# Layer 3's modulation rows: from TensorE fillers in layer 1's attention to GpSimd sums in layer 2's attention

## The reference, cut to what matters

```
shift, scale, gate = jnp.split(jax.nn.silu(c) @ ada_w + ada_b, 3, axis=-1)   # layers 1 and 2; again with c_ctx
h = rmsnorm(x, g_norm) * (1 + scale) + shift
x = x + gate * mixer(h)
...
mod = jax.nn.silu(c_2) @ w_ada[l] + b_ada[l]                                 # layer 3
```

## Time and profile before

| | |
|---|---|
| median of 3 runs (lowest, highest) | 1166.13 us (1163.79, 1166.4) |
| span of the profiled execution, first to last instruction | 1164.7 us |
| busy TensorE / VectorE / ScalarE / GpSimd | 95% / 62% / 56% / 36% |
| chain that ended last | TensorE 77%, VectorE 10%, ScalarE 5%, issue 3%, GpSimd 3%, DMA 2% |
| DMA | 109.33 MB, mean 94 GB/s |
| layer 1's attention | about 103 to 404 us |
| layer 2's attention | about 571 to 753 us |

### The profile page before, as it was taken

One profiled execution on the slowest core, in us unless ns is written; L12 is line 12 of the kernel. 1 busy time (PEld: TensorE's weight loads), 2 busy tenths in 40 slices (PEclk: granted clock), 3 DMA queues, 4 the chain that ended last, 5 costly groups with the idle time before them and its releaser, 6 DMA issues.

```text
span 1164.7 us, 20187 instructions
## 1 busy us (share of the span) xinstructions
PE 1102.9 (95%) x7408; PEld 899.2 (77%) x7408; DVE 726.2 (62%) x1584; ACT 652.1 (56%) x1363; POOL 416.5 (36%) x513
## 2 busy tenths in 40 slices
PE   4899999999998899999999999999999999999996
PEld 0587787878886589888688887798878777888785
DVE  5475665766668725463688788745766775427745
ACT  4614455545556525653577777846567753457733
POOL 1643112111220243676400001416653335456781
PEclk9899999999999999999999999999999999999999
DMA  8732343513113631131201101052312404213112
GB/s 353 270 144 64 111 171 104 187 64 145 46 28 122 228 105 37 37 108 38 57 10 37 64 10 36 13 164 72 87 37 87 150 19 127 91 55 117 47 37 73
DMA packets 34253, 109.33 MB, mean 94 GB/s; under 512 B 4516, under 2 KB 7076, under 8 KB 33772
## 3 DMA queue, kind: packets, MB, share of 16 engines
q1 hardware_dynamic: 34156, 108.05, 27.6%
HBM read 101.39 MB, written 2.11 MB: 89 GB/s over the span
## 4 chain that ended last, share of the span: by engine, by line
PE 77%; DVE 10%; ACT 5%; issue 3%; POOL 3%; DMA 2%; SPq 0%; POOLq 0%; DVEq 0%; ACTq 0%
PE PS L675 31%; PE PS L658 15%; PE PS L791 8%; PE PS L779 7%; PE PS L975 6%; PE PS L1043 3%; PE PS L710 2%; DMA AF<-wstream 2%; PE PS L876 1%; PE PS L691 1%; DVE AD L2364 1%; ACT AF L1267 1%; POOL AR L2545 1%; DVE AF L1982 1%; POOL AR L2561 1%
## 5 line engine op out<-in xcount | busy, mean ns | idle before, releaser
L2545 POOL TENSOR_TENSOR AR<-AF,AR 128x256 fp32r<-128x256 f32 x396 | 301.7, 797 | 596.3 <-ACT AR L1144 596.3
L675 PE MATMUL PS<-AR 128*128 128x512 f32 (+1 forms) x2208 | 450.4, 360 | 4.7 <-POOL AR L2545 1.4
L675 PEld LDWEIGHTS PS<-AR 128*128 128x128 f32 x2208 | 364.0, 189 | 71.8 <-issue 9.7
L658 PE MATMUL PS<-AR 128*128 128x256 f32 (+4 forms) x1284 | 245.5, 327 | 6.7 <-ACT AF L1267 1.7
L658 PEld LDWEIGHTS PS<-AR 128*128 128x128 f32 (+1 forms) x1284 | 180.3, 190 | 42.1 <-issue 21.7
L1276 ACT ACTIVATE AF<-PS 128x512 f32<-128x512 f32 (+3 forms) x192 | 124.6, 649 | 101.1 <-PE PS L779 97.0
L1267 ACT ACTIVATE AF<-PS,AF 128x512 f32<-128x512 f32 (+3 forms) x192 | 140.8, 734 | 27.1 <-DVE AF L2341 18.3
L779 PE MATMUL PS<-AF 128*128 128x128 f32 x864 | 127.7, 275 | 8.3 <-DVE AF L1982 5.7
L1144 ACT ACTIVATE AR<-AF 128x1024 fp32r<-128x1024 f32 x99 | 103.4, 1052 | 41.4 <-PE PS L975 27.9
L779 PEld LDWEIGHTS PS<-AF 128*128 128x128 f32 x864 | 100.2, 140 | 32.6 <-issue 15.5
L791 PE MATMUL PS<-AF 128*64 128x128 f32 x1728 | 115.8, 279 | 3.1 <-DVE AF L1989 2.2
(11 more groups left out here) (213 smaller groups left out, 1136.4 us busy)
## 6 DMA issues: line engine op xcount, KB each, us to landing
AF<-wstream SPq DMA_DIRECT2D x171, 512.0 KB, 5.1
AF<-x_in SPq DMA_DIRECT2D x2, 1024.0 KB, 8.9
AD<-rows SPq DMA_DIRECT2D x4, 512.0 KB, 5.8
out<-AF SPq DMA_DIRECT2D x16, 128.0 KB, 1.9
AF<-AF SPq DMA_DIRECT2D x28, 64.0 KB, 2.0
AF<-rpb_band SPq DMA_DIRECT2D x8, 224.0 KB, 4.9
BIAS<-rpb_band SPq DMA_DIRECT2D x8, 224.0 KB, 4.7
AF<-ctx_in SPq DMA_DIRECT2D x1, 1024.0 KB, 5.8
```

The costliest lines, as they stand in the source:

```text
L658: mm = pe.matmul(out, stationary, moving, start=i == 0, stop=i == len(products) - 1)
L675: mm = pe.matmul(out[:, 0:t1 - t0], a, b, start=k == 0 and i == 0, stop=k == nk - 1 and i == 2)
L2545: ins = pool.tensor_tensor(w[:, 1, at:at + 256], raw(c)[:, at:at + 256], w[:, 0, at:at + 256].bitcast(F32), ALU.subtract)
```

## The change

Layer 3's six blocks leave layer 1's attention. Their chunks stand in the stream behind layer 2's projections, ahead of B.o0. GpSimd takes them one by one: it multiplies each half chunk (128x512) by silu(c_2) of its 128 inputs (one number a partition), adds the two halves, and adds the sum to the block's total (`MIXED`), so that what is left is a sum over the 128 partitions. In step 19 of layer 2's attention TensorE makes that sum for all six blocks (`mixed_rows`, six matmuls with a stationary tile of ones in two columns), VectorE copies it, and the turning `ada2.5.t` follows in step 23. The totals lie where the weight ring for B.o0 to B.o2 is, so ScalarE waits for the turning before it writes these. Layer 2's six blocks are spread anew: one in each of pairs 1, 2, 3 and 5, two in the tail in halves. The roped queries of pairs 2 to 7 move to other places in SyncE's list. Cut:

```diff
 N_CONST = 2
-ADA_GROUPS = {0: ((0, 2), (1, 3), (4, 5)), 1: (tuple(range(6)),), 2: ((0, 1, 2), (3, 4, 5))}
+ADA_GROUPS = {0: ((0, 2), (1, 3), (4, 5)), 1: (tuple(range(6)),), 2: (tuple(range(6)),)}
...
         split(f"A.q{p}", f"A.g{p}")
-        for name in (late_a(p - 1), between_a(p)):
-            if name and not name.endswith(".t"):
-                ada(int(name[3]), int(name[5]))
-    ada(2, 2)
+        name = between_a(p)
+        if name:
+            ada(int(name[3]), int(name[5]))
     split("A.o0")
-    for late in (3, 4, 5):
-        ada(2, late)
+    for late in (4, 5):
+        ada(1, late)
...
           "B.uv", "B.g6", "B.g7", "B.uq1")
+    for b in range(6):
+        ada(2, b)
...
-    return (None, "ada1.0", "ada1.2", "ada1.4", "ada1.5.t", "ada2.1", None, None)[p]
...
-def late_a(p):
-    return (None, "ada1.1", "ada1.3", "ada1.5", "ada2.0", None, None, "ada2.2")[p]
+    return (None, "ada1.0", "ada1.1", "ada1.2", None, "ada1.3", None, None)[p]
...
         late = [f"A.o0.1:{k}" for k in ("02", "24", "45", "56", "67")]
-        return [["ada2.2.t"], ["ada2.3"], ["ada2.4"], ["ada2.5"], ["ada2.5.t"], late[0:1], late[1:3],
+        return [["ada1.4:0"], ["ada1.4:1"], ["ada1.5:0"], ["ada1.5:1"], ["ada1.5.t"], late[0:1], late[1:3],
                 late[3:5]][6 * (p - N_PAIR) + step]
-    gate, between, late = f"A.g{p}.x", between_a(p), late_a(p)
+    gate, between = f"A.g{p}.x", between_a(p)
     out += [[between], [gate]] if between else [[gate + ":0"], [gate + ":1"]]
-    return (out + [[late] if late else []])[step]
+    return (out + [[]])[step]
...
     if step == 3:
-        return []
+        return {5: ["mix2.sum"], 6: ["ada2.5.t"]}.get(p, [])
...
         OB = [tiles(R1, KD, S), tiles(R1[:, KD * S:], KD, S)]
+        MIX = nc.alloc_sbuf_tensor_at("MIX", [P, 7 * S], F32, offset=AR_BASE + 4 * (12288 + 3840 + 6144))
+        MIXED = tiles(MIX, 6, S)
+        ONE_ROW = SILW[:, 0, 0]
...
-            return LOC_[:, 5376:5888]
+            return MIX[:, 6 * S:7 * S] if layer == 2 else LOC_[:, 5376:5888]
...
         sp_x2, ada_used = sem("x_in2"), sem("modulation_chunk_used")
+        mix_step = sem("weighted_rows_step")
...
-        ada_order = [name[:-2] for name, _ in chunks if name.startswith("ada") and name.endswith(".0") and name.count(".") == 2]
+        ada_order = [name[:-2] for name, _ in chunks if name.startswith(("ada0", "ada1")) and name.endswith(".0") and name.count(".") == 2]
+        MIX_STEPS = 6 * 15 + 1
+        def mix_freed(n):
+            halves_added = 1 + 3 * (n + 1) + n - (n + 3) // 4
+            return halves_added + (0 if n % 4 == 0 else 3 if n < 23 else 1)
...
-            def ada_rows(layer, b):
+            def ada_rows(layer, b, k0=0, k1=KD):
                 name = f"ada{layer}.{b}"
-                out = acc_open(name)
+                out = acc_open(name) if k0 == 0 else bank[tasks[name][0]]
                 pe.wait_ge(silc_done, 1)
-                for k in range(KD):
+                for k in range(k0, k1):
...
                         mm.then_inc(ada_used, 1)
-                acc_close(mm, name)
+                if k1 == KD:
+                    acc_close(mm, name)
+            def mixed_rows():
+                out = acc_open("mix2.sum")
+                pe.wait_ge(mix_step, MIX_STEPS)
+                for b in range(6):
+                    g = b % 4
+                    mm = pe.matmul(out[32 * g:32 * g + 12, :], ONE_ROW[:, 10 - 2 * b:22 - 2 * b], MIXED[:, b],
+                                   start=b < 4, stop=b >= 2)
+                acc_close(mm, "mix2.sum")
...
                 out = acc_open(name)
-                rows, i = tasks[f"ada{layer}.{b}"]
+                rows, i = tasks["mix2.sum" if layer == 2 else f"ada{layer}.{b}"]
...
                     project(name, "A.o0", OA, H, T, ready=out_ready(0), k0=int(k[0]), k1=int(k[1]))
+                elif name.startswith("ada") and ":" in name:
+                    piece = int(name[-1])
+                    ada_rows(int(name[3]), int(name[5]), 4 * piece, 4 * piece + 4)
+                elif name == "mix2.sum":
+                    mixed_rows()
...
                             old = in_ring[r - N_SPLIT]
+                            if name in ("B.o0", "B.o1", "B.o2"):
+                                b, i = tasks["ada2.5.t"]
+                                act.wait_ge(acc_ready[b], i)
...
             def ada_part(name):
+                if name == "mix2.sum":
+                    read(dve.tensor_copy(ada_buffer(2, 5), wait_acc(name)), name)
+                    return
...
                 pool.tensor_tensor(QRL[:, i, :], QR[:, i, :], QRH[:, i, :].bitcast(F32), ALU.subtract).then_inc(qr_lo, 1)
+            def mix_rows():
+                b, i = tasks["B.v.5.1"]
+                pool.wait_ge(acc_ready[b], i)
+                done = 1
+                pool.memset(ONE_ROW[:, 10:12], 1.0).then_inc(mix_step, 1)
+                summed = None
+                for b in range(6):
+                    for q in range(4):
+                        c = chunk_at[f"ada2.{b}.{q}"]
+                        w = tiles(raw(c), 2, S)
+                        pool.wait_ge(*raw_loaded(c))
+                        for r in range(2):
+                            pool.tensor_scalar(w[:, r], w[:, r], SILW[:, 1, 2 * q + r, 10:11], None,
+                                               ALU.mult).then_inc(mix_step, 1)
+                        scaled = done + 2
+                        done = scaled
+                        if summed:
+                            add_to(*summed)
+                            done += 1
+                        pool.wait_ge(mix_step, scaled)
+                        total = MIXED[:, b] if q == 0 else w[:, 0]
+                        ins = pool.tensor_tensor(total, w[:, 0], w[:, 1], ALU.add)
+                        ins.then_inc(mix_step, 1)
+                        done += 1
+                        assert q or done == mix_freed(4 * b)
+                        summed = (b, w[:, 0], done) if q else None
+                add_to(*summed)
+                assert done + 1 == MIX_STEPS == mix_freed(23)
+            def add_to(b, part, done):
+                pool.wait_ge(mix_step, done)
+                pool.tensor_tensor(MIXED[:, b], MIXED[:, b], part, ALU.add).then_inc(mix_step, 1)
+            need("B.uq1", 1)
+            mix_rows()
...
                     rows, q = name[:name.rindex(".")], int(name[-1])
-                    if q < 3:
+                    if name.startswith("ada2"):
+                        sp.wait_ge(mix_step, mix_freed(4 * int(name[5]) + q))
+                    elif q < 3:
...
                         sp.wait_ge(acc_ready[b], i)
+            TURN_BEFORE = ("A.g2", "A.g3", "A.g4", "ada1.3.3", "A.g6", "ada1.4.2", "ada1.5.0")
...
                     sp.dma_start(MASK, cst[:, 704:1600]).then_inc(mask_in, 16)
-                for p, before in enumerate(("A.g2", "A.g3", "A.g4", "ada2.0.3", "A.g6", "ada2.2.3", "ada2.3.0"), 1):
+                for p, before in enumerate(TURN_BEFORE, 1):
...
-                if name == "B.o0":
+                if name == "ada2.1.0":
...
                     load_roped_queries(1)
-                for first, after in ((2, "B.o1"), (4, "B.o2"), (6, "B.o5")):
+                for pairs, after in (((2,), "ada2.2.2"), ((3,), "ada2.4.0"), ((4,), "ada2.5.3"), ((5,), "B.o3"), ((6, 7), "B.o5")):
                     if name == after:
-                        load_roped_queries(first)
-                        load_roped_queries(first + 1)
+                        for p in pairs:
+                            load_roped_queries(p)
```

More of the change, by code:

```diff
@@ L247, in filler_chunks @@
         return [f"{name}.{q}" for q in range(4)] if name.count(".") == 1 else []
-    if name.endswith(".rot"):
+    if name.endswith(".rot") or name == "mix2.sum":
         return []
@@ L1447, in evacs_b @@
                     for name in fillers_b(p, s):
-                        if not name.startswith("ada"):
+                        if name[0] == "B":
                             evac_b(name)
@@ L2172, in others_b @@
                     for name in fillers_b(p, s):
-                        ada_part(name) if name.startswith("ada") else low_b(name)
+                        low_b(name) if name[0] == "B" else ada_part(name)
             def out_low_b(j, part):
```

## The result

| | before | after |
|---|---|---|
| median of the runs (lowest, highest) | 1164.96 us (1162.9, 1166.4) | 1187.91 us (1187.77, 1188.55) |
| span of the profiled execution | 1164.7 us | 1186.0 us |
| mean granted TensorE clock | 0.992 | 0.981 |
| division to division of layer 2's attention (first and last start) | 574.0 to 753.4, 179.4 us | 566.2 to 775.0, 208.8 us |

The ratio is 1.020, with an interval of 1.0186 to 1.0215: 23 us slower, outside the forecast range (1159 to 1178). New are L731 (the sum over partitions), L741 (its turning), and on GpSimd L2662 (multiplication), L2671 (adding a chunk's halves) and L2682 (adding to the total).

The account below looks back on a forecast made before the run. TensorE's work and waits were taken as the bound. -6.8 (layer 1's attention) + 2.2 (TensorE, layer 2's) + 0.3 (VectorE's copy and column sums) + 2.5 (delayed divisions) = -1.8 us, from 1166.1 to 1164.3, range 1159 to 1178.

Parts of the forecast that it names:

- The price of a multiplication: GpSimd's chain in layer 2's attention: 0.62 us for each 128x512 multiplication by a column, between 0.61 and 1.30.
- GpSimd is late: Rival: multiplications cost 1.30 us, the chain takes 131 us, TensorE waits 22 us in layer 2's attention; 1183, chance 0.11.
- The point from which it decides: Multiplication price on GpSimd from which its chain is late for TensorE's sum over partitions: 0.85 us.
- The yielding: Time that GpSimd's chain in layer 2's attention loses by giving way to VectorE: 13 us.
- Layer 1's attention: Six modulation blocks and one turning instead of twelve and three there: 6.8 us less, bounds 5.5 and 9.3.
- Pairs 1 to 3: Layer 1's attention, one modulation block instead of two in each gap between pair marks: 2.65 us less together.
- The fourth gap: Layer 1's attention, gap between pair marks from 229.92: it loses a block and a turning, 0.8 us less.
- the term of 1.0: Layer 1's attention: allowance for TensorE's clock not falling at two new gaps without filler, 1.0 us less, between 0 and 2.4.
- TensorE in layer 2's attention: The sum over partitions (up to 1.9 us) and one turning (0.4) add 2.2 us there, bounds 1.4 and 2.3.
- VectorE's lag: Layer 2's attention: divisions wait for GpSimd's instructions and delay TensorE, 0.6 us a pair over 4.2 pairs, 2.5 us.
- VectorE starves: Rival: in layer 2's attention divisions also wait for GpSimd's next instruction, 27 us lost; 1189, chance 0.1.
- The sum: Whole kernel: all terms added, -6.8 + 2.2 + 0.3 + 2.5 = -1.8 us, counted as the same.

Follow-up runs that it names:

- e1: The changed kernel with SyncE loading the queries of pairs 2 to 5 four to eight chunks earlier and pair 6's behind B.o1: 1190.06 us, ratio 1.0221.
- e10: The changed kernel with its 48 multiplications cut from 512 to 256 columns, so half the weighing is not computed: 1163.11 us, ratio 0.9993.
- e3: The changed kernel with each chunk's two TENSOR_SCALAR replaced by one TENSOR_TENSOR with the column broadcast: 1174.37 us, ratio 1.0088.
- e4b: The changed kernel without GpSimd's multiplications, its additions cut to 8 columns, the rows cleared by six small MEMSETs: 1160.26 us, ratio 0.9967.
- e5: The changed kernel with the 48 multiplications deleted and all 42 additions kept, so rows are added unweighted: 1163.94 us, ratio 0.9995.
- e2: e1 with the sum over partitions and the last turning one pair later, and ScalarE's output weight splits in the last three steps: 1168.53 us, ratio 1.0035.
- e7: e2 with one broadcast TENSOR_TENSOR in place of each chunk's two TENSOR_SCALAR: 1173.32 us, ratio 1.0073.

## Why the prediction was wrong, step by step

- **The price of a multiplication** is the step that failed: 0.62 us, bounds 0.61 and 1.30. It is 1.56 at the least and 1.65 in the mean, above my upper bound, so 48 of them took 79.0 us instead of 30. I had drawn it from a cast and from a multiplication of four columns, and held an addition for the ceiling because it has two inputs. Neither row was of this operation in this size, and the ordering "one input costs no more than two" had no row at all. The Trainium skill's "roughly line-rate" for one-input work (GPSIMD Engine Reference, section Engine selection) leant the same way, and the trace disagrees: 1.56 us against 1.28 for the two-input form.
- **The rival "GpSimd is late"** is what happened. Its mechanism, chain, path and size were written down: 131 us for a chain of 134, at the sum or at the fourth pair's queries, 22 us. In after it was 20.6 us at pairs 3 and 4, in e1 24.0 at the sum. Missing were pair 3's queries (I had looked only at the fourth's), the low clock behind each wait (3.6 us), and the chance: 0.11, since I took a bound for a wall. The point from which it decides was put too low at 0.85 us: e10 at 1.09 us a multiplication and e3 at 1.02 for each half chunk are in time for the sum. With after's start, the sum at 679.5 (e10) and 56 us of additions it is (679.5 - 567.8 - 56) / 48 = 1.16 us, yielding included; pair 4's queries come a little sooner, since e10 waits 0.8 us for them at 1.09. The yielding had 13 us in my sum and takes 42 x 0.06 + 48 x 0.09, about 7 (means less the shortest).
- **Layer 1's attention**, -6.8, was -7.0. Pairs 1 to 3 gave 2.5 instead of 2.65. The fourth gap gave 1.7, the 0.8 that I had and 0.9 because the clock stayed full behind its wait at 248.24; at the other new place, behind the last mark, it fell (from 360.21 on). One of two is what the term of 1.0 assumed. The fifth and sixth gap took 0.3 more. The stretch from the last mark to the end of the values gave 3.1 instead of 2.3, and why it gave 0.8 more stays open; that the sum fits this closely is in part luck.
- **TensorE in layer 2's attention**, +2.2, and VectorE's part of it, +0.3: 2.5 together by e4b's stage against before's.
- **VectorE's lag**, +2.5: between 1.9 (e5's stage over e4b's) and 2.7 (e2's, with the whole chain: 187.1 - 181.9, less 1.1 in front of the sum and 1.4 behind ScalarE). The size was right, the reasoning only in part, and so in part by luck: I had a multiplication keep VectorE out for its length, and it doesn't. The rival "VectorE starves" (27 us) did not come. Its evidence, the division of 1.98 us at 574.03, has its like in after at 566.24, behind GpSimd's last splits; the longest behind the chain's own instructions took 1.68. Half of its 27 us came in e3, where the forms were others.
- **The sum**, -1.8, with the chain in time: an estimate gives between -0.5 and -2. e4b gains 3.8 us against the kernel before, and the port takes 1.9 to 2.7 of it by the stages, or 3.0 and 3.3 by the ratios of e10 and e5. Both of these stand at before's time within their intervals (0.9993 and 0.9995), and neither does the whole weighing. No version that does it all was faster than before: e2_late is 4.1 us slower by its ratio, of which its waits in front of the sum and behind ScalarE name 3.1. So whether a gain is left for a chain in time is not shown.

So of +21.3 us of span: -0.8 ahead of layer 1's attention, -7.0 in it, +2.5 for sum and turning, +20.6 for two waits for queries, +3.6 for the clock behind them, +2.1 for the waits for divisions at 661.31 and 699.60 (1.03 and 1.11), -0.3 in the rest: 20.7.

## What to carry to other kernels

Price an operation that moves to another engine by a row of that operation, form and size on that engine; where there is none, an upper bound must not be another form's row, and the chance of "late" has to carry the gap. With a serial chain on a slow engine, list everything that stands behind it in each queue, since the wait comes up at the first of them and not where the result is used. And the shortest form on GpSimd is not the cheapest for the kernel (e7 against e2_late): ask also how long it keeps VectorE's divisions out.

## What the runs showed that I had not expected

- On GpSimd a TENSOR_SCALAR of 128x512 fp32 (1.56 us) is slower than a TENSOR_TENSOR (1.28) and than one with a broadcast operand (1.04 at the shortest).
- How long a division has to wait depends on the form in front of it. Timelines of GpSimd and VectorE in after:

```profile
606.33 3.50 POOL L2662 TENSOR_SCALAR AF<-AF 128x512 f32<-128x512 f32 x2
...
611.04 1.27 POOL L2671 TENSOR_TENSOR AF<-AF 128x512 f32<-128x512 f32 x1
...
606.63 0.80 DVE L2012 TENSOR_SCALAR AF<-AF 128x768 f32<-128x768 f32 x1
...
607.78 0.62 DVE L2012 TENSOR_SCALAR AF<-AF 128x768 f32<-128x768 f32 x1
...
611.23 1.50 DVE L2012 TENSOR_SCALAR AF<-AF 128x768 f32<-128x768 f32 x1
```

The division called 0.30 us into a TENSOR_SCALAR is through 1.10 us after that one's start, before its end, and the next one, called at 607.78 while GpSimd goes from the first TENSOR_SCALAR to the second, isn't held up at all; GpSimd's two are drawn out instead (3.50 us, where a pair takes 3.10 at 688.86). The one called at 611.23, in a TENSOR_TENSOR, is through 0.42 us after that one's end. The Trainium skill (SBUF — State Buffer, section Who interferes with whom) has the loser block for the whole instruction. The trace agrees for TENSOR_TENSOR and MEMSET, and for TENSOR_SCALAR it does not: of the 23 divisions called within one, 18 ended before it. The maximum from PSUM isn't touched: it has a mean of 0.956 us in after and 0.955 in e3. Why the two forms differ is left open.
- A low clock does not follow each wait. After the same wait of 1.68 us the granted clock (the last column but two) stayed full at 248.24 and fell at 321.94, in the windows of after below. This wait in the fourth gap stands in all twelve profiles of the change and its variants, 1.67 or 1.68 us long and behind the same instructions; in six of them a stretch of low clock begins within 2.5 us behind its end, in the other six none does. What decides it is left open.

```profile
246.00:252.00 6.00, 3.92 (x28) 2.99 (x29) 5.72 (x17) 3.80 (x12) 1.75 (x3) 1.00 0.02 4
321.00:327.00 6.00, 4.90 (x25) 3.85 (x26) 4.79 (x17) 4.68 (x15) 2.83 (x4) 0.72 0.00 1
```
